# The expert query projection in rounded passes, and its activations rounded in two halves

## What is computed

```python
def peer_ffn(h, w_q, sub_keys, u_tab, v_tab):
    t = h.reshape(Bt * S, D)
    q = rms_norm((t @ w_q).reshape(n, PEER_HEADS, 2, PEER_D_KEY // 2))
    s = jnp.einsum('thcd,hckd->thck', q, sub_keys)
    ...                       # top 16 of each half, then of the pairs: 16 experts for each token and head
    act = gelu(einsum('td,thkd->thk', t, u_tab[eidx]))
    y = einsum('thk,thkd->td', gates * act, v_tab[eidx])
```

## Time and profile before

| | us |
|---|---|
| median of 3 runs | 2732.45 |
| lowest and highest of them | 2731.07, 2735.79 |
| the profiled execution | 2726.56 |
| its span, first to last instruction | 2724.7 |
| PE busy | 2538.6 (93%) |
| DVE busy | 1612.4 (59%) |
| ACT busy | 947.1 (35%) |
| POOL busy | 783.1 (29%) |

### The profile page before, as it was taken

One profiled execution on the slowest core, in us unless ns is written; L12 is line 12 of the kernel. 1 busy time (PEld: TensorE's weight loads), 2 busy tenths in 40 slices (PEclk: granted clock), 3 DMA queues, 4 the chain that ended last, 5 costly groups with the idle time before them and its releaser, 6 DMA issues.

```text
span 2724.7 us, 47969 instructions
## 1 busy us (share of the span) xinstructions
PE 2538.6 (93%) x17164; PEld 2233.2 (82%) x17164; DVE 1612.4 (59%) x3417; ACT 947.1 (35%) x1627; POOL 783.1 (29%) x586
## 2 busy tenths in 40 slices
PE   5698889999999999999699898899999999999998
PEld 2244779999999999999684334579999999999998
DVE  7999537978898433333441112247968898333333
ACT  1122334344444444444220101034344443444443
POOL 0388726840000222222440000037830000222222
PEclk7699999999999999999799897899999999999999
DMA  8463334443333544444433442034443334444444
GB/s 306 175 217 138 121 126 151 153 137 131 124 131 134 169 166 165 164 167 163 176 109 116 178 161 82 31 134 155 145 141 127 127 128 144 165 166 163 168 162 141
DMA packets 104968, 405.74 MB, mean 149 GB/s; under 512 B 12560, under 2 KB 12816, under 8 KB 101680
## 3 DMA queue, kind: packets, MB, share of 16 engines
q1 hardware_dynamic: 98064, 357.74, 38.3%
q10 hardware_dynamic: 6816, 46.91, 4.6%
HBM read 395.46 MB, written 9.14 MB: 148 GB/s over the span
## 4 chain that ended last, share of the span: by engine, by line
PE 59%; issue 22%; POOL 9%; DVE 8%; ACT 1%; DMA 0%; ACTq 0%; POOLq 0%; DVEq 0%
PE ps L1099 10%; PE ps L1091 10%; PE ps L1095 10%; POOL ring_lo L1685 7%; PE ps L1071 6%; PE ps L1070 6%; PE ps L1074 6%; PE ps L1058 5%; DVE big L1406 2%; POOL ring_lo L1692 1%; PE ps L629 1%; PE ps L969 1%; PE ps L633 1%; PE ps L636 1%; PE ps L965 1%
## 5 line engine op out<-in xcount | busy, mean ns | idle before, releaser
L298 ACT ACTIVATE wt_hi<-ring 128x1024 fp32r<-128x1024 f32 x552 | 581.0, 1053 | 318.2 <-PE ps L969 209.2
L1606 DVE TENSOR_TENSOR ring_lo<-ring,wt_hi 128x1024 fp32r<-128x1024 f32 x256 | 314.7, 1230 | 492.1 <-ACT wt_hi L298 492.1
L1703 POOL TENSOR_TENSOR split<-big,w_hi 128x288 fp32r<-128x288 f32 x256 | 208.1, 813 | 1201.7 <-PE ps L1074 603.3
L1685 POOL TENSOR_TENSOR ring_lo<-ring,wt_hi 128x1024 fp32r<-128x1024 f32 x112 | 307.9, 2756 | 127.5 <-ACT wt_hi L298 127.5
L1070 PE MATMUL ps<-split,wt_hi 128*128 128x288 f32 x1152 | 328.5, 307 | 0.0
L1071 PE MATMUL ps<-split,wt_hi 128*128 128x288 f32 x1152 | 316.1, 298 | 0.0
L1099 PE MATMUL ps<-w_hi,ring_lo 128*128 128x288 f32 x2048 | 313.1, 295 | 1.4 <-DVE ring_lo L1606 1.4
L1095 PE MATMUL ps<-split,wt_hi 128*128 128x288 f32 x2048 | 313.1, 295 | 0.3
L1091 PE MATMUL ps<-w_hi,wt_hi 128*128 128x288 f32 x2048 | 312.9, 295 | 0.0
L1099 PEld LDWEIGHTS ps<-w_hi,ring_lo 128*128 128x128 f32 x2048 | 285.4, 188 | 1.9 <-DVE ring_lo L1606 1.9
L1095 PEld LDWEIGHTS ps<-split,wt_hi 128*128 128x128 f32 x2048 | 285.4, 188 | 0.8 <-POOL split L1703 0.8
(11 more groups left out here) (276 smaller groups left out, 3724.3 us busy)
## 6 DMA issues: line engine op xcount, KB each, us to landing
ring<-in_stream SPq DMA_DIRECT2D x680, 512.0 KB, 3.3
big<-in_kc ACTq DMA_DIRECT2D x8, 1792.0 KB, 7.9
big<-in_vc ACTq DMA_DIRECT2D x8, 1792.0 KB, 7.4
out_qk<-big ACTq DMA_DIRECT2D x1, 3456.0 KB, 10.3
x_keep<-xT ACTq DMA_DIRECT2D x2, 1152.0 KB, 5.5
xT<-x_keep ACTq DMA_DIRECT2D x2, 1152.0 KB, 5.8
out_v<-big ACTq DMA_DIRECT2D x1, 1536.0 KB, 13.9
xT<-in_xT ACTq DMA_DIRECT2D x1, 1152.0 KB, 9.2
```

The lines of the kernel that those rows point to most:

```text
L298: nc.scalar.activation(wt_hi[:, n % 2], ring[:, n % RING], ACT.Copy).then_inc(S["hi_ready"], 1)
L1606: TT(ring_lo[:, s], ring[:, s], wt_hi[:, s % 2].bitcast(F32), ALU.subtract)\
L1685: TT(ring_lo[:, s], ring[:, s], wt_hi[:, s % 2].bitcast(F32), ALU.subtract)\
L1703: TT(w_lo[:, s % 2], W[:, bass.ds(4 * i + s, 1), :].rearrange("p a t -> p (a t)"), w_hi[:, s % 2].bitcast(F32), ALU.subtract).then_inc(S[" ...
```

## The change

The query projection now goes the rounded way. `h_hi` and `h_lo` are made ahead of it, in halves: ACT rounds the first two query tiles, then each half of `modsq` when that half is ready; POOL writes the first half of `h_lo` and DVE the second. PE runs three passes of 8 matmuls for each query tile, and the first tile waits half by half. ACT rounds query tile m + 2 (from m = 6 the first up tiles) ahead of the copy of tile m; POOL writes the rests of the eight query tiles. The store of `x_keep` comes after the second half's rounding. The constants `HI` and `LOU` grow by the eight tiles of each layer.

```diff
-HI = (16, 40 + 256)
-LOU = (16, 40 + PRE)
+HI = (24, 56 + 256)
+LOU = (24, 56 + PRE)
...
-            act.wait_ge(S["h_ready"], 4 * l + 4)
+            for n in range(2):
+                high(act, PQ[l] + n)
+            for n in range(2):
+                act.wait_ge(S["h_ready"], 4 * l + 3 + n)
+                m = slice(4 * n, 4 * n + 4)
+                nc.scalar.activation(h_hi[:, m], modsq[:, m], ACT.Copy).then_inc(S["hh_ready"], 1)
             act.dma_start(x_keep, xT_t[:, :]).then_inc(S["x_out"], 16)
-            nc.scalar.activation(h_hi, modsq, ACT.Copy).then_inc(S["hh_ready"], 1)
 
             for m in range(8):
                 act.wait_ge(S["tile_done"], PQ[l] + m + 1)
+                high(act, PQ[l] + m + 2 if m < 6 else UT[l] + m - 6)
                 nc.scalar.activation(qraw[:, m, :], ps[:, m % 4, 0:T], ACT.Copy).then_inc(S["q_copied"], 1)
-                if m in (5, 6):
-                    high(act, UT[l] + m - 5)
...
-                pe.wait_ge(S["h_ready"], 4 * l + 3)
+                def q_tile(m):
+
+                    n, out = PQ[l] + m, ps[:, m % 4, 0:T]
+                    pe.wait_ge(S["hi_ready"], HI[l] - 8 + m + 1)
+                    for c in range(NC):
+                        if m == 0 and c % 4 == 0:
+                            pe.wait_ge(S["hh_ready"], 2 * l + 1 + c // 4)
+                        mm(out, wt_hi[:, n % 2, c * 128:(c + 1) * 128], h_hi[:, c], start=(c == 0), stop=False)
+                    for c in range(NC):
+                        if m == 0 and c % 4 == 0:
+                            pe.wait_ge(S[("hl_ready", "hl_v")[c // 4]], l + 1)
+                        mm(out, wt_hi[:, n % 2, c * 128:(c + 1) * 128], h_lo[:, c], start=False, stop=False)
+                    pe.wait_ge(S["lo_u"], LOU[l] - 8 + m + 1)
+                    for c in range(NC):
+                        ins = mm(out, ring_lo[:, n % RING, c * 128:(c + 1) * 128], h_hi[:, c], start=False,
+                                 stop=(c == NC - 1))
+                    ins.then_inc(S["tile_done"], 1)
+
                 for m in range(8):
                     if m >= 4:
                         pe.wait_ge(S["q_copied"], 8 * l + m - 3)
-                    wide(PQ[l] + m, m % 4, ps[:, m % 4, 0:T], modsq, h=0 if m else 4 * l + 4).then_inc(S["tile_done"], 1)
+                    q_tile(m)
...
-                pe.wait_ge(S["hh_ready"], l + 1)
-                pe.wait_ge(S["hl_ready"], l + 1)
...
             def peer_dve(l):
+                v.wait_ge(S["hh_ready"], 2 * l + 2)
+                TT(h_lo[:, 4:8], modsq[:, 4:8], h_hi[:, 4:8].bitcast(F32), ALU.subtract).then_inc(S["hl_v"], 1)
...
             def peer_pool(l):
-                pool.wait_ge(S["hh_ready"], l + 1)
-                TT(h_lo, modsq, h_hi.bitcast(F32), ALU.subtract).then_inc(S["hl_ready"], 1)
+                pool.wait_ge(S["hh_ready"], 2 * l + 1)
+                TT(h_lo[:, 0:4], modsq[:, 0:4], h_hi[:, 0:4].bitcast(F32), ALU.subtract).then_inc(S["hl_ready"], 1)
+                with pool.Fori(0, 2) as i:
+                    for s in range(4):
+                        pool.wait_ge(S["hi_ready"], 4 * i + (HI[l] - 8 + s + 1))
+                        TT(ring_lo[:, s], ring[:, s], wt_hi[:, s % 2].bitcast(F32), ALU.subtract)\
+                            .then_inc(S["lo_u"], 1)
                 low_u(l, 0, PRE)
```

More of the change, by code:

```diff
@@ L256, in build @@
             "ss_norm ss_pv oT_ready out_done st_out kv_out glu_used_v "
-            "aq_rc aq_sp hq_ready hq_lo hq_lo_v yh_ready yl_ready s5_bbi ss_oc ss_ot s5_rmr s5_sin s5_zl hi_ready lo_u lo_v hh_ready hl_ready wh_ready wl_ready").split()}
+            "aq_rc aq_sp hq_ready hq_lo hq_lo_v yh_ready yl_ready s5_bbi ss_oc ss_ot s5_rmr s5_sin s5_zl hi_ready lo_u lo_v hh_ready hl_ready wh_ready wl_ready hl_v").split()}
         tile_in = [sem(f"tile_in{s}") for s in range(RING)]
```

## The result

The changed kernel takes 2742.7 us (median of 7 runs, 2740.11 to 2747.11), the kernel before 2732.35 (7 runs, 2730.53 to 2735.79). The ratio is 1.0039, its 95% interval 1.0028 to 1.0051: slower, by more than the 0.2% that a measurement of this kernel can tell from no change. The forecast was 2741.1, in a range of 2735 to 2746. The profiled execution of the changed kernel took 2740.11 us (span 2738.2).

What follows compares the result with a forecast made beforehand. PE, busy 93% of the span, was taken as the bound. Each layer's stretch, 10.85 + 4.75 + 7 x 3.19 = 37.93 us, added 4.49 and 4.17, together +8.7, giving 2741.1 us; range 2735 to 2746.

Steps and rivals of the forecast that it cites:

- Part 1: Query projection, tiles 1 to 7: three rounded passes take 3.19 us a tile against 3.88, gaining 4.8 us a layer.
- The rival that they are not faster: Query tiles: ACT and POOL can't keep up, so 3.88 us a tile, +9.7 us more; chance 0.02.
- Part 2: Start of the first query tile: POOL's instructions hold DVE's second half, so PE resumes at A + 10.85.
- H: End of DVE's last instruction for the second half of the modulated state; forecast at A + 9.60.
- A: Moment in each layer at which DVE finishes the first half of the modulated state; start of the compared stretch.
- Rivals 1 and 2: At the second half: DVE not held, 2728.3 us, chance 0.07; only two POOL instructions hold DVE, 2737.0 us, chance 0.09.
- Part 3: First query tile after PE resumes: 4.75 us with the clock at first low, bounds 4.15 to 5.0.
- Part 4: Behind E: DVE's squares come later, ending by E + 6.5; PE wants them at E + 6.55, so no cost.
- E: First weight load of up tile 0 in each layer; end of the compared stretch.
- Rival 3: Behind E: DVE also held by POOL's rest of up tile 2, squares late, 2745.8 us; chance 0.05.
- The sum: Stretch from A to E: 10.85 + 4.75 + 7 x 3.19 = 37.93 us a layer; together +8.7 us.

Runs made afterwards that it cites:

- The run with the gap filled: The changed kernel plus 14 plain matmuls nobody reads, between PE's first four matmuls of query tile 0 and its wait for the second half; 2740.18 us.
- The last run: The kernel before plus 13 plain matmuls nobody reads, behind the sum of squares ahead of the expert stage; 2731.78 us, ratio 0.9999.

## Why the prediction was right, step by step

**Part 1, the matmuls.** Expected 3.19 a tile; 3.12 in layer 0 (393.53 - 371.69 over seven), 3.22 in layer 1 (1823.91 - 1801.38; 3.20 without the start of its tile 1, which still ran at the lower clock). Right; feeding them costs nothing from the second tile on. The rival that they are not faster did not happen. Why there are two paces, 3.12 and 3.20, at a granted clock of 1.00 in both, stays open. Over seven tiles it makes 0.6 us, so a difference of that size in a single layer says nothing of an edit.

**Part 2, the start.** Expected H at A + 9.60 and PE 1.25 behind it; H came at A + 9.70 and PE 1.25 behind. The mechanism, one DVE instruction for each POOL instruction in the row, holds for two, three and four of them. One item was wrong: the prediction had three of the four scale-and-shift instructions held. In fact the small multiply ahead of them, L1384, was the first (2.74 us where undisturbed it takes 0.29), and two of the four came next. The multiply began at A + 1.30 in both stages. In the attention POOL began at A + 1.35, between the multiply and the first L1368 (0.16 us ahead of it); here it began at A + 1.27, 0.03 us ahead of the multiply. The attention's row of the multiply, before the change:

```profile
1311.52 0.29 DVE L1366 TENSOR_TENSOR big<-big,ada 128x128 f32<-128x128 f32 x1
```

So the prediction took over from another stage an order that less than a tenth of a us decides, without saying so. That H still came within 0.1 us is in part luck. POOL's row ended 0.24 us earlier than forecast, at A + 8.58 and not 8.82 (it began 0.08 earlier, and its first subtraction took 2.62 us, not 2.73), but two scale-and-shift instructions were left behind it (0.72 us) where the prediction had one (0.32). The Trainium skill (SBUF — State Buffer, section "Who interferes with whom") gives tensor_tensor with two SBUF inputs as contending with GpSimd's reads too, and the trace agrees (2.74 us). It also says that whoever issues first holds the other: the trace agrees with that as well, POOL's subtraction took 3.78 us instead of 2.62 where DVE was 0.04 us ahead. Rows of this case limit it: in the first norm the same scale-and-shift took 0.77 us at most, with a POOL instruction (L1639, TENSOR_SCALAR) of 1.64 us beside it, so it was not blocked to that one's end. Which POOL instructions hold DVE was not tested beyond these subtractions.

**Rivals 1 and 2.** DVE not held at all would have given H at A + 3.21: seen only where POOL was silent. Two held, H at A + 7.54: seen only where POOL had two instructions in the row (A + 7.70, and +4.5 us in the stage, which is what that rival said). Both fall by the changed kernel's own rows and are put there at will by the edits.

**Part 3, tile 0 and the clock.** Expected 4.75 (4.15 to 5.0); 4.60 and 4.73 to the first weight load of tile 1. The low level ended at about 371.5 in layer 0, 4.4 us behind the resumption (expected 3.4 to 5.1). The run with the gap filled shows that the clock is the reason: from matmul to matmul 3.08 us without the gap, a wait of 0.3 included, and 4.73 with it.

**Part 4, what is moved.** The squares were to end by E + 6.5 and PE to want them at E + 6.55. The timeline behind E in layer 0, against the earlier trace rows:

```profile
395.00 2.40 POOL L1705 TENSOR_TENSOR ring_lo<-ring,wt_hi 128x1024 fp32r<-128x1024 f32 x1 [0.72 <-ACT wt_hi L298]
...
395.25 4.57 DVE L1475 TENSOR_TENSOR big<-big 128x2304 f32<-128x2304 f32 x1 [26.82 <-ACT big L316]
...
398.21 3.83 POOL L1705 TENSOR_TENSOR ring_lo<-ring,wt_hi 128x1024 fp32r<-128x1024 f32 x1 [0.81 <-ACT wt_hi L298]
...
399.96 1.78 PEld L1014 LDWEIGHTS ps<-big,consts 128*128 128x128 f32 x8
```

The squares take 4.57 us where they took 2.56, and start 0.25 us behind POOL's L1705. They end at 399.82, E + 6.29; PE takes them at 399.96, E + 6.43. No wait, with a cover of 0.14 us. Rival 3, the squares late, missed by little: they started 0.25 us behind one rest and 2.96 us ahead of the next (398.21), which they held in turn (3.83 us). PE lost nothing by that either: behind E, up tiles 1 and 2 come at 3.21 and 8.25 us, before the change at 3.35 and 8.38.

**The sum.** Expected 37.93 a layer; 37.39 and 38.22, together +8.41 against the expected +8.7. By parts in layer 0: seven tiles gained 7 x 0.76 = 5.3 us, the start and tile 0 lost 9.3 (10.95 + 4.60, against 33.44 - 7 x 3.88 = 6.28). The prediction had 4.8 and 9.1. In layer 1 the gain is 4.6, by the slower pace.

**What stays open.** The medians differ by 10.35, 1.9 more than the stretches. The profiled executions differ by 13.5, 5.1 more; of that, 2.9 lie between layer 0's E and layer 1's A, in code that the change leaves alone. That span was 1389.3 us in the profiled execution of before, 1392.2 in the changed kernel's, and between 1390.5 and 1401.5 in the seven others. The traces tell where these two part: from layer 0's A to the norm ahead of the attention (DVE's RECIPROCAL, at 1304.93 before and 1309.98 after) the changed kernel is 3.7 us later, about what its stretch costs, and from there to layer 1's A it took 475.7 us against 472.5. The last run, whose code there is that of the kernel before but for its 13 matmuls at the end, took 476.7. So these 3 us need no cause in the change; they vary from one execution to the next, and the one of before was the shortest. Whether a part of the 1.9 in the medians belongs to the change was not separated.

## To carry to other kernels

An edit that makes the bound engine's work cheaper is worth nothing until its first operand is there: cost the start of the stage apart from its steady state, and ask of every helper instruction which other engine it holds while it runs. Here the same matmuls made the kernel 10 us slower or 5 us faster, depending on whether POOL's subtractions ran in a row beside the last instructions of DVE's second half or DVE did that work itself behind them. When the trace has the same code in another stage, take its durations, but say which starts were a close race there, since a few hundredths of a us decide which engine is held.

## What the runs showed of the hardware that was not expected

- An instruction of 0.29 us is held as long as a large one: 2.74 us behind a POOL subtraction that began 0.03 us earlier. Beside these subtractions, what a held instruction costs is set by the other engine's instruction, not by its own size.
- Between POOL subtractions that follow each other without a break exactly one DVE instruction gets through each time, in all of the rows of two, three and four, ending about 0.15 us behind POOL's.
- It goes the other way too: with DVE 0.04 us ahead, POOL's 2.62 us became 3.78, and it was PE that paid: those 1.16 us are a part of its wait of 2.53.
- For a subtraction of 128 x 1024, POOL takes 2.39 us and DVE 1.2 (2.35 for two): the work moved from POOL to DVE was not only out of the way, it was halved.
